# A fused mixer, PEER and transformer kernel: 768 instead of 640 gathered features, the high products of a unit ahead of its low ones, and loads and PSUM copies moved

## The chip, the cores and the metric

The kernel runs on one core of one Trainium2 chip. The metric is the device time of one execution in microseconds (us), and lower is better. Before the change, three runs took 2994.68, 3000.39 and 3007.38 us, median 3000.39. The profiled execution is a run of its own.

## The reference, cut to what matters

256 tokens of 2048 features go through two blocks, in fp32. The first block mixes the tokens (a pooling part and a recurrent part), then runs a PEER layer: each token picks 16 of 16384 experts in each of 8 heads, so 128 experts in all. The second block is attention, a convolution and a feed-forward part of 8192. The change concerns the PEER layer's second product:

```python
        gate = jax.nn.softmax(top_s, axis=-1)
        u = jnp.take(peer_u, expert, axis=0)
        act = jax.nn.gelu(jnp.einsum('chkd,cd->chk', u, zc))
        v = jnp.take(peer_v, expert, axis=0)
        w = (gate * act.astype(jnp.float32)).astype(zc.dtype)
        return jnp.einsum('chk,chkd->cd', w, v).astype(zc.dtype)
```

The result for one token is a sum of 128 rows of `peer_v`, each with its own weight. It can be computed in two ways: as a dense product of all 16384 experts with a weight matrix that is zero where an expert was not picked, or by gathering the 128 rows of each token and adding them up with their weights. The kernel does most of it densely and a part by gathering.

## The kernel before, in words

**Units and halves.** All matrix work is cut into 544 units. A unit has two halves of weights, each 128 partitions x 1024 fp32 values (512 KB). For every half, SP issues a DMA into one of 8 `raw` slots as soon as the half that used the slot 8 halves earlier has been multiplied; ACT rounds it into one of 7 `hi` slots (`prep`, L982); DVE subtracts that from the raw half and leaves the rest, `lo`, in the raw slot (L1378). PE multiplies in three products for accuracy: high by high, low by high, high by low. Each engine's program is written out in order, one unit after the other: the tables of the file (`LOAD_G_AT`, `LOAD_H_AT`, `COPY_AT`, `PHASED` and so on) say at which unit an engine issues each extra operation. Semaphores count finished steps (`s_raw`, `s_hi`, `s_lo`, `s_mm`).

**Stages.** Units 0 to 55 are the first block's projections. Units 56 to 183 are the PEER layer's first products (`u` stage, 8 chunks of 16 units), and units 184 to 311 its second products (`v` stage, again 8 chunks). Unit 312 (`F0`) starts the second block.

**The second products.** Here the output is by token: 128 tokens on the partitions, features in the columns. A unit holds four blocks of 128 experts by 512 features. Token half 0 multiplies all 512 columns. Token half 1 multiplies only the first 128 x `FROM_Q` of the 2048 features (`FROM_Q` = 11, 1408 features), and the other `WIDE` = 640 are gathered. So with q the quarter of 512 features: units of q = 0 and 1 have 512 columns for both halves, units of q = 2 have 512 and 384, units of q = 3 have 512 and nothing. Chunks 0 to 6 go through q = 0, 1, 2, 3 four times, and the last chunk has four units of q = 0, then four of q = 1, 2 and 3. A `FLIPPED` unit has its halves in `hi` slots 6 and 0, so that a piece of 384 columns can't be read in one stride: there it is cut into 256 and 128 (`pieces`). This concerns five units of q = 2.

**The gather.** `widen` (L1178, on ACT's DMA queue) copies the 640 features of all 16384 experts into a table `v_wide`, one row per expert, in 80 copies of 512 KB, at the units in `COPY_AT`. In the `v` stage, POOL issues for each of the 128 picks one indirect DMA that gathers 128 rows (L2102, into a ring of 6 blocks of two picks) and one for their activations (L2110, `asp`), 13 DMAs in 6 units. DVE adds the rows up (`picked_dot`, L1709), four units behind.

**Gates and activations.** For each chunk of the `v` stage, ACT's queue loads the gates `Gc` (L1186, four times 512 KB) and the activations (`A`, `Y` <- `h_scratch`, L1196, four times 512 KB). DVE multiplies them, ACT and DVE split them into `ZB`.

**The end of the stage.** The quarters are finished one after another in the last chunk. ACT and DVE copy them out of the PSUM (`expert_out`: ACT's copy is L1132; DVE's is L1761, and L1765 puts the gathered features in), PE transposes them (`expert_turn`, L715), DVE adds them to X (L1771), ACT squares and scales X (`expert_sum`, L1138 to L1146) and DVE makes the low part `ZA` (L1775), which unit 312 multiplies.

## Time and profile before

| | us |
|---|---|
| median of three runs | 3000.39 |
| the three runs | 2994.68, 3000.39, 3007.38 |
| profiled execution, its own time | 2997.14 |
| its span in the profile | 2995.3 |
| PE busy | 2971.8 |
| DVE busy | 2145.3 |
| ACT busy | 1565.0 |
| POOL busy | 961.1 |

The span is the time from the first to the last instruction of the profile, and the profiled execution's own time has 1.84 us around it. A busy PE is not a PE at its peak: matmuls overlap, so the pitch from one start to the next is what a matmul costs, and the duration in a row is longer. "PEclk" is the clock that TensorE was granted, as a share of its full 2.4 GHz. The "DMA share" of a stretch is the mean busy share of the core's 16 DMA engines; transfers that overlap on one engine can take it a little above 1. "q1" is the queue of SP's loads, "q10" that of ACT's, "q0" that of POOL's gathers.

### The profile page before, as it was taken

To read this page: it belongs to the slowest core of one execution; us is meant where nothing else is said; L and a number is where in the kernel's file an instruction comes from. 1 tells how busy PE (TensorE), PEld (TensorE's weight loads), DVE (VectorE), ACT (ScalarE), POOL (GpSimd) and SP (SyncE) were. 2 spreads that over 40 slices of the span, in tenths; PEclk is the share of its full clock that TensorE was granted. 3 is DMA by queue.
4 is the path that set the end of the run, shared out by engine and by line. 5 is a ranking of instruction groups with operands and counts; after the bars stand their busy time and mean duration, and the time that the engine had idled before them with its cause. 6 is when DMAs were issued, how large, how long until landed. Compare 5 with 4: busy or idle time off the path is not lost.

```text
span 2995.3 us, 42127 instructions
## 1 busy us (share of the span) xinstructions
PE 2971.8 (99%) x15968; PEld 2559.2 (85%) x15968; DVE 2145.3 (72%) x3097; ACT 1565.0 (52%) x2160; POOL 961.1 (32%) x728
## 2 busy tenths in 40 slices
PE   9999999999999999999999999999999999999999
PEld 8888888888888888888788788888888888888887
DVE  8957995555566767887778899897867855545554
ACT  7655464444444544545455656656566544434443
POOL 0022458888883055565554300000522000000000
PEclk9999999999999999999999999999999999999999
DMA  8898978999999899999997555555555565577664
GB/s 301 289 323 285 350 217 246 270 245 247 246 244 281 283 308 337 347 334 343 333 333 255 198 179 175 171 182 189 190 189 176 188 187 191 189 206 193 193 194 148
DMA packets 403194, 730.44 MB, mean 244 GB/s; under 512 B 66992, under 2 KB 226992, under 8 KB 400304
## 3 DMA queue, kind: packets, MB, share of 16 engines
q1 hardware_dynamic: 240608, 574.70, 58.8%
q10 hardware_dynamic: 111184, 110.88, 11.2%
q0 software_dynamic: 51200, 42.17, 6.5%
q8 instruction: 126, 2.06, 0.3%
q14 instruction: 76, 0.62, 0.1%
HBM read 690.80 MB, written 78.78 MB: 257 GB/s over the span
## 4 chain that ended last, share of the span: by engine, by line
PE 88%; DVE 4%; DMA 3%; issue 2%; ACT 1%; POOL 1%; SPq 0%; ACTq 0%; POOLq 0%; DVEq 0%
PE G L586 40%; PE G L590 20%; DMA raw<-in_pv 3%; PE G L656 3%; PE G L657 3%; PE G L658 3%; PE M L656 2%; PE M L658 2%; PE M L657 2%; PE G L683 2%; PE M L683 2%; PE M L684 2%; PE G L684 2%; PE M L685 2%; PE G L685 2%
## 5 line engine op out<-in xcount | busy, mean ns | idle before, releaser
L586 PE MATMUL G<-ZA,hi 128*128 128x512 f32 x5098 | 1765.7, 395 | 4.0 <-DVE lo L1378 1.5
L1378 DVE TENSOR_TENSOR lo<-raw,hi 128x1024 fp32r<-128x1024 f32 x1088 | 1338.1, 1244 | 515.7 <-ACT hi L982 485.3
L982 ACT ACTIVATE hi<-raw 128x1024 fp32r<-128x1024 f32 x1088 | 1129.9, 1055 | 615.5 <-DMA raw<-in_pv 276.6
L590 PE MATMUL G<-ZA,lo 128*128 128x256 f32 x5114 | 1389.4, 278 | 0.0
L586 PEld LDWEIGHTS G<-ZA,hi 128*128 128x128 f32 x5098 | 943.1, 188 | 211.0 <-DVE lo L1378 2.2
L590 PEld LDWEIGHTS G<-ZA,lo 128*128 128x128 f32 x5114 | 961.0, 188 | 16.7
L2086 POOL DMA_INDIRECT g_scratch<-sel,IDX x256 | 442.2, 1728 | 115.5 <-issue 82.6
L989 ACT ACTIVATE tA<-G 128x256 f32<-128x256 f32 x367 | 139.2, 380 | 508.9 <-PE G L590 488.3
L1384 DVE TENSOR_TENSOR tS<-G,tA 128x256 f32<-128x256 f32 x336 | 140.7, 419 | 262.0 <-ACT tA L989 256.7
L2102 POOL DMA_INDIRECT vrow<-v_wide,IXV x128 | 166.0, 1297 | 241.9 <-PE G L590 127.4
L656 PE MATMUL G<-hi,ZB 128*128 128x512 f32 (+3 forms) x532 | 197.9, 372 | 3.8 <-DVE lo L1378 3.8
L2110 POOL DMA_INDIRECT asp<-h_scratch,IXA x128 | 161.2, 1260 | 119.4 <-PE G L658 51.0
L657 PE MATMUL G<-lo,ZB 128*128 128x512 f32 (+3 forms) x532 | 197.8, 372 | 0.0
L658 PE MATMUL G<-hi,ZB 128*128 128x512 f32 (+3 forms) x532 | 197.6, 371 | 0.0
L586 PE MATMUL G<-ZB,hi 128*128 128x512 f32 x512 | 177.4, 394 | 1.4 <-DVE ZB L1458 1.4
L656 PE MATMUL M<-hi,ZB 128*128 128x512 f32 x384 | 151.5, 394 | 3.3 <-DVE lo L1378 3.3
L657 PE MATMUL M<-lo,ZB 128*128 128x512 f32 x384 | 150.4, 392 | 0.0
L658 PE MATMUL M<-hi,ZB 128*128 128x512 f32 x384 | 150.4, 392 | 0.0
L590 PE MATMUL G<-ZB,lo 128*128 128x256 f32 x512 | 140.9, 277 | 0.0
L1794 DVE SCALAR_TENSOR_TENSOR CV<-UC,col,CV 128x256 f32<-128x256 f32 x240 | 117.0, 488 | 6.6
L656 PEld LDWEIGHTS G<-hi,ZB 128*128 128x128 f32 x532 | 99.9, 188 | 22.1 <-DVE lo L1378 5.5
L586 PEld LDWEIGHTS G<-ZB,hi 128*128 128x128 f32 x512 | 95.6, 188 | 23.5 <-DVE ZB L1458 1.7
(368 smaller groups left out, 2779.1 us busy)
## 6 DMA issues: line engine op xcount, KB each, us to landing
raw<-in_pu SPq DMA_DIRECT2D x256, 512.0 KB
raw<-in_pv SPq DMA_DIRECT2D x256, 512.0 KB
raw<-in_w_in SPq DMA_DIRECT2D x192, 512.0 KB
raw<-in_w_up SPq DMA_DIRECT2D x128, 512.0 KB
raw<-in_w_down SPq DMA_DIRECT2D x128, 512.0 KB
v_wide<-in_pv ACTq DMA_DIRECT2D x80, 512.0 KB
raw<-in_w_out SPq DMA_DIRECT2D x32, 512.0 KB
raw<-in_wq SPq DMA_DIRECT2D x32, 512.0 KB
```

The source lines that it names most:

```text
L586: pe.matmul(G[:, 0:512], w, Z[:, k, :], start=first, stop=False, skip_group_check=True)
L590: m = pe.matmul(G[:, 0:256], lo[raw_slot(POS[u][p])][:, k % 8, :], weights(u, p)[1][:, k, 0:256], start=False, stop=last, skip_group_check ...
L656: pe.matmul(to, zhi, vhi, start=c == 0 and n == 0 and x == 0, stop=False, skip_group_check=True)
L657: pe.matmul(to, zhi, vlo, start=False, stop=False, skip_group_check=True)
L658: m = pe.matmul(to, zlo, vhi, start=False, stop=c == 7 and n == 3 and x == 3, skip_group_check=True)
L982: act.activation(hi[w][:, :, :], raw[r].rearrange("p (k n) -> p k n", k=8), ACT.Copy).then_inc(s_hi, 1)
L989: act.activation(tA[b % 3][:, :], GB[b % 4][:, 256:512], ACT.Copy).then_inc(s_low, 1)
L1378: dve.tensor_tensor(lo[r][:, :, :], raw[r].rearrange("p (k n) -> p k n", k=8), hi[w][:, :, :].bitcast(F32), ALU.subtract).then_inc(s_lo, 1)
L1384: dve.tensor_tensor(dst, GB[b % 4][:, 0:256], tA[b % 3][:, :], ALU.add).then_inc(s_join, 1)
L2086: pool.indirect_dma_start(scr, bass.IndirectOffsetOnAxis(IDX[:, t, k:k + 1], 0), sel[:, t, k:k + 1], None, compute_op=ALU.add).then_inc(s_ ...
L2102: pool.indirect_dma_start(vrow[:, slot_of(b), k, :], None, vwide, bass.IndirectOffsetOnAxis(IXV[:, at:at + 1], 0)).then_inc(s_pick[b % 2], 16)
L2110: pool.indirect_dma_start(asp[:, at:at + 1], None, hflat, bass.IndirectOffsetOnAxis(IXA[:, at:at + 1], 0)).then_inc(s_pick[b % 2], 16)
```

## The change: what it does

- `WIDE` goes from 640 to 768, so `FROM_Q` from 11 to 10. Units of q = 2 multiply 512 and 256 columns. Gathers, dots and the table become one fifth wider. `RING` goes from 6 blocks to 5. The table takes 96 copies instead of 80: 52 of them in units 4 to 39 where there were 46, and 45 in units 66 to 154 (every second unit) where there were 34 in units 66 to 165 (every third).
- `expert_unit` issues all products with high weights (zhi x vhi and zlo x vhi) of a unit first, waiting only for `s_hi`, and then all products with low weights, for which it waits for `s_lo`. `pieces` goes: 256 columns can always be read in one stride.
- Group 3 of the gates is loaded at units 178 to 181, ahead of the stage; groups 4 to 7 come at units 196, 201, 206, ... to 274, seven units behind the place that the group before had, so that no `Gc` load stands at the same unit as a load of activations.
- `PHASED` gains the second unit of each chunk of the `u` stage (8 units): its matmuls are the same, in an order that has two high products before the first low one.
- PE's third `expert_turn` comes behind unit 309 instead of 308. ACT's last `expert_out` comes at unit 310 instead of 312.

```diff
-PHASED = [19, OT + 1, MG, YO + 1, M0 + 3, M0 + 5]
+PHASED = [b + 1 for b in UB] + [19, OT + 1, MG, YO + 1, M0 + 3, M0 + 5]
...
-WIDE = 640
+WIDE = 768
...
-RING = 6
+RING = 5
...
-for _n, _u in enumerate(sorted(list(range(4, 40)) + list(range(8, 28, 2)) + list(range(66, 168, 3)))):
+for _n, _u in enumerate(sorted(list(range(4, 40)) + list(range(8, 38, 2)) + list(range(66, 156, 2)))):
...
-                               (LOAD_G_AT, 2, _m - 11), (KEPT_AT, 2, _m - 8)):
+                               (LOAD_G_AT, 2, _m - 11), (KEPT_AT, 2, _m - 8), (LOAD_G_AT, 3, _m - 6)):
...
-    for _table, _u in ((LOAD_G_AT, _u), (LOAD_H_AT, _u), (KEPT_AT, _u + 5)):
-        _table[_u] = [(3 + _j // 4, _j % 4)]
+    for _table, _group, _u in ((LOAD_H_AT, 3 + _j // 4, _u), (KEPT_AT, 3 + _j // 4, _u + 5), (LOAD_G_AT, 4 + _j // 4, _u + 7)):
+        if _group < KEPT:
+            _table[_u] = [(_group, _j % 4)]
...
+TURN_AT = (V_LAST + 4, V_LAST + 8, V_LAST + 13)
...
-                weights_ready(POS[u][1])
...
-                for x in range(4):
-                    if q == 0 and x % 2 == 0:
-                        pe.wait_ge(s_za, 8 * c + 2 * n + x // 2 + 1)
...
-                        for at, w, vhi, vlo in pieces(u, whi, wlo, x, e):
-                            to = G[:, at:at + w]
-                            pe.matmul(to, zhi, vhi, start=c == 0 and n == 0 and x == 0, stop=False, skip_group_check=True)
-                            pe.matmul(to, zhi, vlo, start=False, stop=False, skip_group_check=True)
-                            m = pe.matmul(to, zlo, vhi, start=False, stop=c == 7 and n == 3 and x == 3, skip_group_check=True)
+                pe.wait_ge(s_hi, POS[u][1] + 1)
+                for low in range(2):
+                    if low:
+                        weights_ready(POS[u][1])
+                    for x in range(4):
+                        if q == 0 and x % 2 == 0 and not low:
+                            pe.wait_ge(s_za, 8 * c + 2 * n + x // 2 + 1)
...
+                            if low:
+                                m = pe.matmul(G[:, 0:e], zhi, vlo, start=False, stop=c == 7 and n == 3 and x == 3, skip_group_check=True)
+                            else:
+                                pe.matmul(G[:, 0:e], zhi, vhi, start=c == 0 and n == 0 and x == 0, stop=False, skip_group_check=True)
+                                pe.matmul(G[:, 0:e], zlo, vhi, start=False, stop=False, skip_group_check=True)
                 m.then_inc(s_mm, 2)
...
-                if u in range(V_LAST + 4, F0, 4):
-                    expert_turn((u - V_LAST) // 4 - 1)
+                if u in TURN_AT:
+                    expert_turn(TURN_AT.index(u))
...
-                if u in range(V_LAST + 4, F0 + 1, 4):
+                if u in range(V_LAST + 4, F0, 4):
                     expert_out((u - V_LAST) // 4 - 1)
...
+                if u == V_LAST + 14:
+                    expert_out(3)
```

On PE, in unit 186 (the first of q = 2; G and M are the PSUM banks of the two token halves, `hi` and `lo` on the left of ZB the weights, and L656, L657, L658 the three products), the kernel before has for one block of experts after another, with three rows for each token half:

```order
5965 L656 MATMUL G<-hi,ZB 128x512
5966 L657 MATMUL G<-lo,ZB 128x512
5967 L658 MATMUL G<-hi,ZB 128x512
5968 L656 MATMUL G<-hi,ZB 128x384
5969 L657 MATMUL G<-lo,ZB 128x384
5970 L658 MATMUL G<-hi,ZB 128x384
```

and the changed kernel, at the unit's first matmuls and at the change from high to low:

```order
5970 L652 MATMUL G<-hi,ZB 128x512
5971 L653 MATMUL G<-hi,ZB 128x512
5972 L652 MATMUL G<-hi,ZB 128x256
5973 L653 MATMUL G<-hi,ZB 128x256
...
5982 L652 MATMUL G<-hi,ZB 128x512
5983 L653 MATMUL G<-hi,ZB 128x512
5984 L652 MATMUL G<-hi,ZB 128x256
5985 L653 MATMUL G<-hi,ZB 128x256
5986 L650 MATMUL G<-lo,ZB 128x512
5987 L650 MATMUL G<-lo,ZB 128x256
5988 L650 MATMUL G<-lo,ZB 128x512
5989 L650 MATMUL G<-lo,ZB 128x256
```

The low product (L650) of each block moved to behind all sixteen high ones (L652, L653), and the 384 columns of token half 1 became 256.

On ACT, near the start of the `v` stage, the kernel before issues a load of gates (L1186) and one of activations (L1196) at the same unit, with the splits L982 of the weights around them:

```order
937 L982 ACTIVATE hi<-raw 128x1024 x2
938 L1186 DMA Gc<-g_scratch 128x1024
939 L1196 DMA A<-h_scratch 128x1024
940 L982 ACTIVATE hi<-raw 128x1024 x6
941 L1106 ACTIVATE ZB<-A 128x2x256 x2
942 L982 ACTIVATE hi<-raw 128x1024 x4
943 L1186 DMA Gc<-g_scratch 128x1024
944 L1196 DMA A<-h_scratch 128x1024
```

and the changed kernel at the same place:

```order
952 L977 ACTIVATE hi<-raw 128x1024 x8
953 L1101 ACTIVATE ZB<-A 128x2x256 x2
954 L977 ACTIVATE hi<-raw 128x1024 x2
955 L1191 DMA A<-h_scratch 128x1024
956 L977 ACTIVATE hi<-raw 128x1024 x6
957 L1101 ACTIVATE ZB<-A 128x2x256 x2
958 L977 ACTIVATE hi<-raw 128x1024 x4
959 L1191 DMA A<-h_scratch 128x1024
960 L977 ACTIVATE hi<-raw 128x1024 x4
961 L1101 ACTIVATE ZB<-A 128x2x256 x2
962 L1181 DMA Gc<-g_scratch 128x1024
```

The two loads are now seven units apart, and the first load of gates comes two units behind the second of activations.

On ACT, at the end of the stage, `expert_sum` is the group of four rows L1138 to L1146 for one tile of 128 features, and the last copy out of the PSUM (L1132) comes in the kernel before behind the groups of tiles 10 and 11:

```order
1097 L982 ACTIVATE hi<-raw 128x1024 x2
1098 L1138 ACTIVATE tQ<-X 128x256
1099 L1139 ACTIVATE X<-X,col 128x256
1100 L1143 ACTIVATE ZA<-X,col 128x256
1101 L1146 ACTIVATE tQ<-X 128x256
1102 L982 ACTIVATE hi<-raw 128x1024 x2
1103 L1138 ACTIVATE tQ<-X 128x256
1104 L1139 ACTIVATE X<-X,col 128x256
1105 L1143 ACTIVATE ZA<-X,col 128x256
1106 L1146 ACTIVATE tQ<-X 128x256
1107 L1132 ACTIVATE A<-M 128x512
```

In the changed kernel the same stretch reads:

```order
1120 L977 ACTIVATE hi<-raw 128x1024 x2
1121 L1127 ACTIVATE A<-M 128x512
1122 L1133 ACTIVATE tQ<-X 128x256
1123 L1134 ACTIVATE X<-X,col 128x256
1124 L1138 ACTIVATE ZA<-X,col 128x256
1125 L1141 ACTIVATE tQ<-X 128x256
1126 L977 ACTIVATE hi<-raw 128x1024 x2
1127 L1133 ACTIVATE tQ<-X 128x256
1128 L1134 ACTIVATE X<-X,col 128x256
1129 L1138 ACTIVATE ZA<-X,col 128x256
1130 L1141 ACTIVATE tQ<-X 128x256
```

The copy (now L1127) stands ahead of both groups and of the two splits between them.

## Rows read from the trace of the kernel before

**Rows 1.** The page: busy us of each engine, and the chain's shares:

```profile
PE 2971.8 (99%) x15968; PEld 2559.2 (85%) x15968; DVE 2145.3 (72%) x3097; ACT 1565.0 (52%) x2160; POOL 961.1 (32%) x728
...
PE 88%; DVE 4%; DMA 3%; issue 2%; ACT 1%; POOL 1%; SPq 0%; ACTq 0%; POOLq 0%; DVEq 0%
```

**Rows 2.** Stretches: window, us, busy of PE, PEld, DVE, ACT, POOL, clock, DMA share, GB/s:

```profile
1070.00:1610.00 540.00, 532.88 (x2437) 445.80 (x2436) 428.54 (x483) 268.36 (x284) 313.80 (x246) 1.00 0.95 335
560.00:960.00 400.00, 400.00 (x2309) 349.79 (x2308) 236.18 (x290) 198.31 (x288) 308.08 (x182) 1.00 0.94 249
```

**Rows 3.** Waits between 1070 and 1610 us (us in all, times, longest):

```profile
ACT hi L982 <- DMA raw<-in_pv: 257.2, 185, 7.3
...
POOL asp L2110 <- DVE vacc L1709: 15.3, 9, 3.8
...
PE G L656 <- DVE lo L1378: 3.8, 4, 1.5
PE M L656 <- DVE lo L1378: 3.3, 5, 1.2
```

**Rows 4.** PE's timeline, a unit of q = 2 (start, us):

```profile
1141.87 0.33 PE L656 MATMUL G<-hi,ZB 128*128 128x384 f32 x1
...
1142.40 0.40 PE L656 MATMUL G<-hi,ZB 128*128 128x512 f32 x1
...
1142.86 0.39 PE L658 MATMUL G<-hi,ZB 128*128 128x512 f32 x1
```

**Rows 5.** PE's timeline, a flipped unit of q = 2:

```profile
1160.41 0.28 PE L656 MATMUL G<-hi,ZB 128*128 128x256 f32 x1
...
1160.76 0.22 PE L656 MATMUL G<-hi,ZB 128*128 128x128 f32 x1
...
1161.05 0.44 PE L656 MATMUL G<-hi,ZB 128*128 128x512 f32 x1
```

**Rows 6.** PE's group of 384 columns, 1056 to 1640 us:

```profile
L657 PE MATMUL G<-lo,ZB 128*128 128x384 f32 x98 | 33.3, 340 | 0.0
```

**Rows 7.** DMA, 1070 to 1610 us: packets, MB, share of 16 engines; issues:

```profile
q1 hardware_dynamic: 61626, 118.79, 63.9%
q0 software_dynamic: 13856, 40.71, 20.5%
q10 hardware_dynamic: 5760, 20.97, 10.0%
...
Gc<-g_scratch ACTq DMA_DIRECT2D x20, 512.0 KB
A<-h_scratch ACTq DMA_DIRECT2D x12, 512.0 KB
Y<-h_scratch ACTq DMA_DIRECT2D x8, 512.0 KB
```

**Rows 8.** View of stretches, short ones inside the second products:

```profile
1360.00:1370.00 10.00, 10.00 (x47) 8.40 (x46) 6.24 (x9) 4.11 (x5) 5.99 (x5) 1.00 1.03 393
1236.00:1266.00 30.00, 30.00 (x138) 25.34 (x137) 22.91 (x28) 13.23 (x14) 18.50 (x16) 1.00 0.99 360
```

**Rows 9.** DVE's groups between 1070 and 1610 us (busy, mean ns, idle before):

```profile
L1709 DVE SCALAR_TENSOR_TENSOR vacc<-vrow,asp,vacc 128x640 f32<-128x640 f32 x118 | 99.2, 882 | 2.1
```

**Rows 10.** DMA queues between 560 and 960 us:

```profile
q10 hardware_dynamic: 35449, 23.45, 19.6%
...
v_wide<-in_pv ACTq DMA_DIRECT2D x24, 512.0 KB
```

**Rows 11.** PE's waits at the stage's end, 1610 to 1690 us:

```profile
PE G L715 <- DVE A L1765: 3.1, 1, 3.1
PE M L715 <- ACT A L1132: 2.4, 1, 2.4
```

**Rows 12.** ACT's timeline at the stage's end:

```profile
1664.06 0.42 ACT L1138 ACTIVATE tQ<-X 128x256 f32<-128x256 f32 x1 [2.53 <-DVE X L1771]
...
1674.09 0.58 ACT L1132 ACTIVATE A<-M 128x512 f32<-128x512 f32 x1
```

More of the change, by code:

```diff
@@ L623, in half @@
                     x += step
-            def pieces(u, whi, wlo, x, e):
-                if e % 256 == 0:
-                    return [(0, e, whi[:, 0:e // 256, :, x, :], wlo[:, 0:e // 256, :, x, :])]
-                if FLIPPED[u]:
-                    return [(0, 256, whi[:, 0, :, x, :], wlo[:, 0, :, x, :]), (256, 128, whi[:, 1, 0, x, :], wlo[:, 1, 0, x, :])]
-                a, b = POS[u][0] % NW, POS[u][0] % NRAW
-                whi, wlo = (w.rearrange("p s t f -> p (s t) f").rearrange("p (q k) f -> p q k f", k=4)
-                            for w in (his[:, a:a + 2, :, :], los[:, b:b + 2, :, :]))
-                return [(0, e, whi[:, 0:e // 128, x, :], wlo[:, 0:e // 128, x, :])]
             def expert_unit(u):
@@ L645, in expert_unit @@
                 whi, wlo = (w.rearrange("p s (q k) f -> p s q k f", k=4) for w in (whi, wlo))
-                for x in range(4):
-                    if q == 0 and x % 2 == 0:
-                        pe.wait_ge(s_za, 8 * c + 2 * n + x // 2 + 1)
-                    for h, G in enumerate(VM[q]):
-                        e = min(512, max(0, 128 * (FROM_Q - 4 * q))) if h else 512
-                        if not e:
-                            continue
-                        zhi, zlo = (ZB[:, 4 * n + x, at:at + 128] for at in (128 * h, 256 + 128 * h))
-                        for at, w, vhi, vlo in pieces(u, whi, wlo, x, e):
-                            to = G[:, at:at + w]
-                            pe.matmul(to, zhi, vhi, start=c == 0 and n == 0 and x == 0, stop=False, skip_group_check=True)
-                            pe.matmul(to, zhi, vlo, start=False, stop=False, skip_group_check=True)
-                            m = pe.matmul(to, zlo, vhi, start=False, stop=c == 7 and n == 3 and x == 3, skip_group_check=True)
+                pe.wait_ge(s_hi, POS[u][1] + 1)
[5 more added lines that the diff above has]
+                            pe.wait_ge(s_za, 8 * c + 2 * n + x // 2 + 1)
+                        for h, G in enumerate(VM[q]):
+                            e = min(512, max(0, 128 * (FROM_Q - 4 * q))) if h else 512
+                            if not e:
+                                continue
+                            zhi, zlo = (ZB[:, 4 * n + x, at:at + 128] for at in (128 * h, 256 + 128 * h))
+                            vhi, vlo = whi[:, 0:e // 256, :, x, :], wlo[:, 0:e // 256, :, x, :]
+                            if low:
[3 more added lines that the diff above has]
+                                pe.matmul(G[:, 0:e], zlo, vhi, start=False, stop=False, skip_group_check=True)
                 m.then_inc(s_mm, 2)
```

## The prediction, made before the changed kernel ran

> **What bounds the kernel now.** I read the page's busy times and its chain first. PE is busy 2971.8 of 2995.3 us and makes up 88% of the chain that ended last [rows 1], so time is won only where PE has fewer columns to multiply or stops waiting, and only as long as what feeds PE keeps up. Then the view of stretches, because the average hides the stage that the change touches. In the stretch from 1070 to 1610 us (units 187 to 300, the second products) PE is busy 532.88 of 540.00 us at full clock, while the 16 DMA engines are busy to 0.95 and move 335 GB/s. From 560 to 960 us (first products) PE is busy 400.00 of 400.00 at a DMA share of 0.94 and 249 GB/s [rows 2]. The third view is the one of waits: in the second products ACT waits 257.2 us for raw weights, in 185 waits, so a half is split as soon as it has landed. What PE waits for is the low part, nine times, 3.8 and 3.3 us in all, never above 1.5 us [rows 3]. So this stage is PE-bound with the DMA close behind it. There are two questions: how many PE columns go, and whether the DMA can bring the same weights, and more gathered rows, in the shorter time.
>
> **PE's side.** Only units of q = 2 change. In an ordinary one, three matmuls of 384 columns run from 1141.87 to 1142.40, 0.177 us each [rows 4]. Three of 256 run from 1160.41 to 1160.76 in a flipped unit, 0.117 each, and its three of 128 take until 1161.05, so the six take 0.64 us [rows 5]. After, three of 256 do it. An ordinary unit has four blocks of three: 12 x (0.177 - 0.117) = 0.72 us. A flipped one gains 4 x (0.64 - 0.35) = 1.16 us. The stage has 32 units of q = 2, five of them flipped, so 27 with 384 columns: each of their three products has 98 records, where 27 x 4 = 108 were issued and a few are missing from the trace [rows 6]. Inside 1070 to 1610 stand 23 ordinary and 4 flipped units; one ordinary is unit 186, before it, and the four of the last chunk (304 to 307) come after it. So PE gains 23 x 0.72 + 4 x 1.16 = 16.6 + 4.6 = 21.2 us there. The new order of products lets a unit start with `s_hi` alone and puts the wait for the low part behind two thirds of its matmuls, 1.8 us (q = 3) to 3.6 us (q = 0 and 1) later at 0.23 us for 512 columns (1142.40 to 1142.86 for two [rows 4]). The longest of the nine waits is 1.5 us, so at an equal supply all 7.1 us go, and what is late next is the high part. The matmuls themselves are as many as before, and a changed order costs nothing by itself; I bound that at 0.1 us either way for a unit. PE alone would need 540.0 - 21.2 - 7.1 = 511.7 us.
>
> **The DMA's side.** The shares in the stretch are 63.9% for the weights, 20.5% for POOL's gathers and 10.0% for ACT's loads [rows 7], 94.4% of 540, that is 510 us of all 16 engines. The rows gathered get a fifth wider. That adds between 0 (if the cost is per row; the activations' gathers on the same queue don't grow) and 0.2 x 20.5% x 540 = 22 us (all by bytes). I take 22, since the queue's 40.71 MB are nearly all these rows. Loads of gates: 4 of the 40 loads of ACT's queue (20 of `Gc`, 12 and 8 of A and Y) move ahead of the stage, - 4/40 x 10.0% x 540 = - 5. Sum 527 us. To fit into 511.7 us the share would have to be 527 / 511.7 = 1.03, for 500 us on end. The trace has such a share for 10 us (1.03 at 393 GB/s), while the best 30 us that I found have 0.99 [rows 8], and the whole stretch has 0.95. So the price of this term lies between three points. With a share of 0.95 as before the stretch takes 527 / 0.95 = 555 us (+15). With 1.00 it takes 527 us (-13). With 1.03 PE decides and it takes 511.7 (-28). I take 1.00: PE set the pace before, so the 0.95 was demand and no ceiling; the later wait for the low parts and the loads that no longer coincide allow a longer queue; and 1.00 is nearest to the 30 us row. The stretch gives **-13**.
>
> By the Trainium skill, DMA: Bandwidth & Descriptors, section Where 436 GB/s comes from, HBM gives a core some 358 GB/s. The bytes of the stretch are 118.79 + 40.71 + 20.97 = 180.5 MB, and with a fifth more gathered rows and four loads fewer 186.5 MB, an estimate by that page of 521 us, so -19 instead of -13. The trace agrees as far as a mean of 335 goes, and has 393 for 10 us, so as a ceiling for short stretches the figure doesn't hold here.
>
> **Wider rows elsewhere.** DVE has 118 dots of 882 ns there [rows 9]; at a fifth wider, 0.18 us more at most (all of it by columns), 128 x 0.18 = 23 us over the stage. DVE is busy 428.54 of 540 [rows 2]: 428.5 + 21 = 450 of 527, hidden behind its idle time, and delays of the low parts lie inside the 1.8 to 3.6 us that the new order gives. With the old order they would have gone to PE. At the end of the stage a pair of dots and the wider add stand on DVE's path: +0.4. Unit 186 gives -0.7, a flipped 304 -1.2.
>
> **Copies of the table.** 11 more fall into the first products, every second unit in place of every third. All of ACT's queue has 19.6% of 400 us there = 78 us, with 24 copies in it besides other traffic [rows 10], so a copy costs at most 3.3 us and the 11 at most 36 us; they are issued over 88 units, some 490 us (2309 matmuls in 400 us at 32 for a unit make 5.5 us a unit [rows 2]), and would lift the share from 0.94 to at most 1.01. I take half. PE doesn't wait there in 400 us [rows 2], so 0; if the cover is gone, up to +10. The five more copies in the first block: 0 to +3, taken 0.
>
> **The ring of 5, the loads of gates, PHASED.** A pick waits for the dots of the block five before in place of six. Blocks come every 1.85 units (13 DMAs in 6 units, 4 for a block) and dots four units behind, so the slot is free 5 x 1.85 - 4 = 5.2 units (some 25 us) ahead; POOL waited for dots 15.3 us in 9 waits, 3.8 at most [rows 3]. 0, bounds 0 and +2. The gates' load sits on ACT ahead of splits; at its new unit its slot is longer free than before: 0, bounds -2 and +1 (the first of them beyond what the DMA term has). The 8 new PHASED units have the same matmuls: 0, bounds -1 and +1.
>
> **End of the stage.** PE waited 3.1 us for DVE's copy ahead of the third transposes and 2.4 us for ACT's last copy [rows 11]. With the transposes a unit of q = 3 later (2.7 us) the first wait nearly goes, and PE has unit 309 done sooner. But the end of this stage is the chain of copies, adds and `expert_sum`, which feeds unit 312: ACT stood idle until DVE's add at 1664.06 and copied the last bank at 1674.09 [rows 12]. PE's time saved in 305 to 311 is given back there, so those three q = 2 units count 0. The last copy moves ahead of two groups of four instructions of about 0.4 us each and of splits; DVE's add of that bank stands where it stood. I take 0, bounds -4 (the last bank is ready so much sooner) and +3 (ACT stands at the copy until unit 311 is done and its groups are late).
>
> **Sum.** -13 - 0.7 - 1.2 + 0.4 = -14.5. From the profiled execution's 2997.14 us (span 2995.3 and 1.8 around it) this is 2982.6. The profiled run lies 3.25 us below the median of 3000.39, so against that median 2985.9. I predict **2985 us**, between the two.
>
> **Rivals.** (1) *The DMA keeps up and PE decides.* For it: the 10 us rows at 1.03, and that shares above 1 only mean overlapping transfers. Against it: nothing in the trace holds it for 30 us. Time: -28 in place of -13, 2968 to 2971 us. (2) *The DMA has no more than its mean, slower.* The place is the same stretch: the weights' queue shares engines with a fifth more gathered bytes; from a share below 527 / 540 = 0.976 the stage is longer than before, and at 0.95 it is +15 - 1.5: 3011 to 3014 us. For it: the share is 0.95 and ACT already waits for weights half the stretch. Against it: 0.99 for 30 us with PE never waiting in them. (3) *The cover in the first products or at the stage's end is gone:* copies at +10 or ACT's copy at +3 beside the -14.5: some 2991 to 2998 us. (4) *The change doesn't do what it says:* the low waits turn into waits for the high parts one for one, so the 7.1 us stay and the share stays near 0.97: 2998 us, no change.
>
> **Chances.** Forecast (share 0.98 to 1.02): 0.45. Rival 1: 0.24. Rival 2: 0.12. Rivals 3 and 4 together: 0.19. A measurement of this kernel can tell 0.5%, 15 us, from no change, so faster means below some 2985. The forecast sits on that bound and gives 0.22 to each side, rival 1 is all faster, rival 2 mostly slower: faster 0.46, same 0.43, slower 0.11. The range leaves out the outer half of rival 1 and of rival 2: 2964 to 3007 us. The forecast's own range (share 0.98 to 1.02) is 2975 to 2996.
>
> **What would show it.** Right: PE has no 384-column group; the units of q = 2 are 0.7 us shorter; the stretch of units 187 to 300 lasts some 527 us with a DMA share near 1.00; PE's waits are for ACT's `hi` or few for `lo`; the first products keep 400.00 of 400.00. Rival 1 shows as a stretch of 512 us without waits, rival 2 as PE waits of over 30 us in it with a share still at 0.95. Wrong altogether would be waits in the first products, or a stage's end that is longer by more than 3 us.

## The result: 2969.5 us, one per cent faster, twice the gain forecast

Four runs of the changed kernel took 2967.06 to 2971.44 us, median 2969.48, against a median of 2999.88 us before (four runs). The ratio is 0.9895 with a 95% interval of 0.9875 to 0.9914. The forecast was 2985, so its sign was right, the size half of what came, and the numbers are those of rival 1. The profiled execution took 2971.44 us, 25.7 us less than the one before (2997.14).

The page of the profile after, for [rows 1] (busy us of each engine, and the chain's shares):

```profile
PE 2946.2 (99%) x15908; PEld 2535.8 (85%) x15908; DVE 2160.1 (73%) x3097; ACT 1567.5 (53%) x2160; POOL 984.2 (33%) x728
...
PE 89%; DVE 4%; DMA 2%; issue 2%; ACT 1%; POOL 1%; SPq 0%; ACTq 0%; POOLq 0%; DVEq 0%
```

PE is still the bound, with 25.6 us less of it. Where they went shows in ACT's timeline: the first split of unit 188 and that of unit 300, first in the kernel before, then after.

```profile
1065.27 1.06 ACT L982 ACTIVATE hi<-raw 128x1024 fp32r<-128x1024 f32 x1 [3.37 <-DMA raw<-in_pv]
...
1596.84 1.06 ACT L982 ACTIVATE hi<-raw 128x1024 fp32r<-128x1024 f32 x1 [0.24 <-DMA raw<-in_pv]
```

```profile
1065.71 1.06 ACT L977 ACTIVATE hi<-raw 128x1024 fp32r<-128x1024 f32 x1 [3.20 <-DMA raw<-in_pv]
...
1570.85 1.06 ACT L977 ACTIVATE hi<-raw 128x1024 fp32r<-128x1024 f32 x1 [0.43 <-DMA raw<-in_pv]
```

From 531.6 us the distance fell to 505.1: 26.4 us, the whole difference and 0.7 more. So the stretch that was 1070 to 1610 us is 1070 to 1584 us now. The view of stretches after, for [rows 2], with one piece of 85 us:

```profile
1070.00:1584.00 514.00, 509.13 (x2389) 424.44 (x2389) 442.63 (x483) 268.04 (x284) 340.99 (x247) 1.00 1.01 364
...
1245.00:1330.00 85.00, 85.00 (x404) 71.14 (x403) 76.65 (x84) 46.51 (x50) 53.87 (x42) 1.00 1.03 377
```

```profile
560.00:960.00 400.00, 400.00 (x2308) 349.70 (x2308) 239.51 (x292) 200.41 (x290) 305.29 (x183) 1.00 0.95 259
```

The first products are as they were: 400.00 us of 400.00, with the denser copies at a DMA share of 0.95 after 0.94. In the second products the DMA engines held 1.01 and 364 GB/s for 514 us, and for 85 us 1.03 and 377 GB/s with no wait of PE. The waits in that stretch, for [rows 3] (us in all, times, longest):

```profile
ACT hi L977 <- DMA raw<-in_pv: 245.4, 196, 4.7
...
PE M L652 <- ACT hi L977: 2.5, 4, 1.0
PE M L650 <- DVE lo L1375: 2.4, 2, 1.5
POOL asp L2107 <- DVE vacc L1706: 2.1, 3, 1.5
```

PE waits 4.9 us where it waited 7.1, now half for the high part. POOL waits less for dots with the smaller ring, not more. The DMA queues there, for [rows 7], and DVE's dots, for [rows 9]:

```profile
q1 hardware_dynamic: 61729, 119.00, 65.7%
q0 software_dynamic: 13856, 48.84, 24.9%
q10 hardware_dynamic: 5184, 18.88, 9.6%
```

```profile
L1706 DVE SCALAR_TENSOR_TENSOR vacc<-vrow,asp,vacc 128x768 f32<-128x768 f32 x118 | 115.0, 1016 | 2.1
```

A dot takes 0.134 us more (0.18 was the bound). POOL's queue moves the fifth more. At the stage's end PE's waits are, for [rows 11]:

```profile
PE G L588 <- DVE lo L1375: 4.7, 1, 4.7
PE G L710 <- DVE A L1758: 2.9, 1, 2.9
PE G L588 <- DVE ZA L1772: 1.3, 2, 0.7
```

The wait for ACT's last copy (2.4 us) is gone, and a wait of 4.7 us for the low part of unit 312 has come. PE's clock fell at this end as well. The view of stretches has these two after, and under them the only one of its kind there before:

```profile
1611.00:1616.00 5.00, 4.59 (x20) 4.15 (x21) 4.96 (x7) 2.12 (x2) 0.00 (x0) 0.66 0.41 156
1642.00:1650.00 8.00, 5.68 (x23) 5.01 (x24) 6.23 (x7) 7.94 (x15) 4.45 (x5) 0.57 0.18 72
```

```profile
1659.00:1663.00 4.00, 4.00 (x15) 3.23 (x14) 4.00 (x5) 1.76 (x2) 0.00 (x0) 0.57 0.38 153
```

The granted clock is the mean of a stretch in which it stood partly at 2.4 and partly at 1.2 GHz. Each of the three lies at a long wait of PE: 2.9 us until 1611.41 and 4.7 us until 1644.32 after, 3.15 us until 1658.43 before. From unit 299 to the program's end the profiled execution takes 1.4 us more than before, though four units of q = 2 with fewer columns lie in it.

### The profile page after: what moved, and what is told of

It reads as the page before. It is cut to its first block, busy times and chain, and to the rows that moved or that the text cites. A ratio compares the mean times of both kernels' runs of the same rounds, so it can differ in the third digit from the quotient of the medians.

```text
span 2969.6 us, 42024 instructions
## 1 busy us (share of the span) xinstructions
PE 2946.2 (99%) x15908; PEld 2535.8 (85%) x15908; DVE 2160.1 (73%) x3097; ACT 1567.5 (53%) x2160; POOL 984.2 (33%) x728
## 4 chain that ended last, share of the span: by engine, by line
PE 89%; DVE 4%; DMA 2%; issue 2%; ACT 1%; POOL 1%; SPq 0%; ACTq 0%; POOLq 0%; DVEq 0%
PE G L588 40%; PE G L592 20%; PE M L650 3%; PE G L652 3%; PE G L653 3%; PE G L650 3%; PE M L652 3%; PE M L653 3%; DMA raw<-in_pv 2%; PE G L679 2%; PE M L679 2%; PE M L680 2%; PE G L680 2%; PE M L678 2%; PE G L678 2%
## 5 line engine op out<-in xcount | busy, mean ns | idle before, releaser
L2099 POOL DMA_INDIRECT vrow<-v_wide,IXV x128 | 179.6, 1403 | 218.1 <-PE G L592 129.2
L2107 POOL DMA_INDIRECT asp<-h_scratch,IXA x128 | 173.8, 1358 | 91.6 <-PE G L650 33.4
L652 PE MATMUL G<-hi,ZB 128*128 128x512 f32 (+1 forms) x512 | 182.1, 364 | 0.0
L653 PE MATMUL G<-hi,ZB 128*128 128x512 f32 (+1 forms) x512 | 180.3, 364 | 0.0
L652 PE MATMUL M<-hi,ZB 128*128 128x512 f32 x384 | 150.2, 391 | 2.5 <-ACT hi L977 2.5
L653 PE MATMUL M<-hi,ZB 128*128 128x512 f32 x384 | 149.6, 390 | 0.0
L1706 DVE SCALAR_TENSOR_TENSOR vacc<-vrow,asp,vacc 128x768 f32<-128x768 f32 x126 | 123.5, 1021 | 2.2
L650 PE MATMUL G<-lo,ZB 128*128 128x512 f32 (+1 forms) x512 | 112.8, 362 | 0.0
L653 PEld LDWEIGHTS G<-hi,ZB 128*128 128x128 f32 x512 | 96.8, 189 | 16.9
```

Of the source, the lines that this page charges most:

```text
L650: m = pe.matmul(G[:, 0:e], zhi, vlo, start=False, stop=c == 7 and n == 3 and x == 3, skip_group_check=True)
L652: pe.matmul(G[:, 0:e], zhi, vhi, start=c == 0 and n == 0 and x == 0, stop=False, skip_group_check=True)
L653: pe.matmul(G[:, 0:e], zlo, vhi, start=False, stop=False, skip_group_check=True)
L2099: pool.indirect_dma_start(vrow[:, slot_of(b), k, :], None, vwide, bass.IndirectOffsetOnAxis(IXV[:, at:at + 1], 0)).then_inc(s_pick[b % 2], 16)
L2107: pool.indirect_dma_start(asp[:, at:at + 1], None, hflat, bass.IndirectOffsetOnAxis(IXA[:, at:at + 1], 0)).then_inc(s_pick[b % 2], 16)
```

## Experiments

They were measured in three groups of four, in the order in which they stand here, each group on one chip and together with runs of the kernel before (the first and the third group on the same chip). Within a group the times can be set against each other to some 2 us; the kernel before had a median of 2998.84, 2997.46 and 2998.72 us in them. The changed kernel itself ran ahead of them, in none of the groups.

**1. The order of products alone, on the kernel before.**

```diff
-                weights_ready(POS[u][1])
+                pe.wait_ge(s_hi, POS[u][1] + 1)
+                for low in range(2):
+                    if low:
+                        weights_ready(POS[u][1])
...
```

> The kernel before with one part of the change: the products with high weights of a unit first, then those with low weights, behind their own wait. Columns, gather, loads and the stage's end as before. Theory A (the order takes the nine low waits and nothing else): the 7.1 us of waits in the second products go, 2993 us, 0.2% faster, PE waits for low parts gone there. Rival (the high part is as late as the low one was): the waits only change their name, 3000 us.

Median 2990.65 us (12 runs), before 2998.84 in this group: ratio 0.9981 (0.9968 to 0.9993, which is 2 to 10 us). The profile has no wait of PE in the second products at all. Theory A holds, 7 us forecast and 8 measured. Four of the twelve runs took 3000.6 to 3002.5, the other eight 2988.7 to 2992.7, and the profiled one is among the four; more on that in the last section.

**2. The old order on the changed kernel.**

```diff
-                pe.wait_ge(s_hi, POS[u][1] + 1)
-                for low in range(2):
-                    if low:
-                        weights_ready(POS[u][1])
...
+                weights_ready(POS[u][1])
+                for x in range(4):
...
+                        pe.matmul(to, zhi, vhi, start=c == 0 and n == 0 and x == 0, stop=False, skip_group_check=True)
+                        pe.matmul(to, zhi, vlo, start=False, stop=False, skip_group_check=True)
+                        m = pe.matmul(to, zlo, vhi, start=False, stop=c == 7 and n == 3 and x == 3, skip_group_check=True)
```

> The changed kernel with the order of products of before (high-high, high-low, low-high for each block, one wait for the low part at the unit's start); everything else as changed. Theory A (PE's columns decide, the DMA engines have room, and the order is worth about the waits that were there): 5 to 8 us longer than the changed kernel, some 2976 us. Theory B (at a DMA share above 1.00 landings come so late that the low parts are late in far more units, and the later wait is what hides it): 15 us or more longer, 2985 us or above, with more than 20 us of PE waits for low parts in the second products.

2987.78 us (6 runs), ratio 0.996 (0.9945 to 0.9975), 18 us above the changed kernel and 17 above the fourth kernel of the same group. PE's waits in this execution, and the stretch:

```profile
PE M L647 <- DVE lo L1371: 16.2, 19, 2.5
```

```profile
1070.00:1584.00 514.00, 500.21 (x2324) 413.59 (x2323) 430.92 (x469) 260.55 (x275) 324.73 (x240) 1.00 0.99 355
```

Theory B has the time, though its row of waits is below 20 us: 19 waits, 16.2 us, none longer than 2.5. The changed kernel has 4.9 us. The rest of the 15 us by which the two profiled executions differ is not seen in the rows of waits, but it hangs on them: a wait costs more than its row shows (see the table behind experiment 12), and one of 2.33 us is followed by matmuls at half the clock:

```profile
1370.10 0.63 PE L647 MATMUL M<-hi,ZB 128*128 128x512 f32 x1 [2.33 <-DVE lo L1371]
```

```profile
1370.00:1375.00 5.00, 4.90 (x14) 3.87 (x15) 3.39 (x4) 2.11 (x2) 1.98 (x2) 0.66 0.97 366
```

The order, which I had priced at 7.1 us, is worth 17 or 18 at the new pace. Waits of 2.5 us at most lie mostly within the 1.8 to 3.6 us that the later wait gives.

**3. The gates' loads where they were.**

```diff
-                               (LOAD_G_AT, 2, _m - 11), (KEPT_AT, 2, _m - 8), (LOAD_G_AT, 3, _m - 6)):
+                               (LOAD_G_AT, 2, _m - 11), (KEPT_AT, 2, _m - 8)):
...
+    for _table, _u in ((LOAD_G_AT, _u), (LOAD_H_AT, _u), (KEPT_AT, _u + 5)):
+        _table[_u] = [(3 + _j // 4, _j % 4)]
```

> The changed kernel with the loads of gates where they were before: groups 3 to 7 inside the stage, at the same units as the loads of activations. Theory A (the engines have room): 0 to 2 us longer than the changed kernel. Rival (two loads of 512 KB at once are what makes the weights late): 5 us or more longer, with PE waits in units 189 to 288 near the loads.

2973.98 us (5 runs), ratio 0.9913 (0.9898 to 0.9929). That is 2.9 us above the fourth kernel and 4.5 above the changed one, between theory A and its rival, and the intervals of the three overlap. Its profile shows 1.7 us of waits for the high part and 1.8 us for the low in the second products, fewer than the 4.9 of the changed kernel, and units 185 to 299 take 520.4 us where the changed kernel takes 520.9. The 1.9 us by which this execution is the longer one lie ahead of that: by the end of unit 184 it is 2.5 us late, 1.5 us of it by unit 56, and in that first block the view of stretches has the clock at 0.66 from 166 to 171 us (1.00 in the changed kernel), behind a wait of 1.99 us for ZB. So no cost of the loads' place is shown; the medians bound it at some 3 to 4 us.

**4. The stage's end as before.**

```diff
-TURN_AT = (V_LAST + 4, V_LAST + 8, V_LAST + 13)
+TURN_AT = (V_LAST + 4, V_LAST + 8, V_LAST + 12)
...
-                if u in range(V_LAST + 4, F0, 4):
+                if u in range(V_LAST + 4, F0 + 1, 4):
...
-                if u == V_LAST + 14:
-                    expert_out(3)
```

> The changed kernel with the third transposes behind unit 308 and ACT's last PSUM copy at unit 312, as before. My step (the chain of copies, adds and sums sets the end of the stage, PE's order doesn't): within 1 us of the changed kernel. Rival (the earlier copy is what won): 2 to 4 us longer. In the profile: the wait at the third transposes is 3 us or more again, and ACT's last copy comes some 3 us later.

2971.13 us (5 runs), ratio 0.99 (0.9884 to 0.9915), 1.6 us above the changed kernel, which is between the step and its rival and within what runs of different groups differ. The waits are those of before and longer, and still cost nothing that can be measured (from unit 299 to the end 1389.2 us against 1388.3):

```profile
PE G L710 <- DVE A L1760: 5.3, 1, 5.3
PE G L710 <- DVE A L1756: 3.3, 1, 3.3
PE M L710 <- ACT A L1127: 2.4, 1, 2.4
```

**5. 640 gathered, everything else as changed.**

```diff
-WIDE = 768
+WIDE = 640
...
-RING = 5
+RING = 6
...
+                            for at, w, vhi, vlo in pieces(u, whi, wlo, x, e):
```

> The changed kernel with 640 gathered features, a ring of 6 and the 80 copies of before; 384 columns in units of q = 2, pieces again, everything else as changed (order of products, gates' loads, PHASED, end). Both theories: PE's columns are back, 23 x 0.72 + 4 x 1.16 + 2 = 23 us longer than the changed kernel, some 2991 us, and like the order alone on the kernel before.

2988.93 us (11 runs), ratio 0.9969 (0.996 to 0.9978). It is 21 us above the eighth kernel, of the same group, where 23 were forecast.

**6. The bytes without the columns.**

```diff
-                                e = min(512, max(0, 128 * (FROM_Q - 4 * q))) if h else 512
+                                e = (512, 512, 384, 0)[q] if h else 512
```

> The changed kernel, 768 features gathered, but units of q = 2 still multiply 384 columns of the second token half (the 128 columns too many are computed and not used). Against the kernel with 640 and 384 this adds the bytes and nothing for PE. Theory A (the DMA engines have room at this pace): the same within 1.5 us, some 2991 us, DMA share near 0.99. Theory B (more gathered bytes make weights late in themselves): 4 us or more longer than it.

2990.45 us (12 runs), ratio 0.9977 (0.9967 to 0.9986): 1.5 us more than with 640. At this pace a fifth more gathered bytes cost next to nothing, at a share of 0.99 after 0.97. In the profiled executions units 185 to 299 take 538.5 us with either; what the wider rows cost (3.2 us there) lies behind unit 299. Theory A.

**7. The columns without the bytes.**

```diff
-WIDE = 768
+WIDE = 640
...
+                                e = (512, 512, 256 if c else 384, 0)[q] if h else 512
```

> The changed kernel with 640 gathered features, a ring of 6 and 80 copies, but units of q = 2 multiply only 256 columns of the second token half from chunk 1 on; features 1280 to 1407 of that half get the products of chunk 0 alone, the rest of them is left out. This takes PE's columns without the bytes. Theory A (PE decides, the bytes cost nothing): 20 x 0.72 + 4 x 1.16 = 19 us shorter than the kernel with 640 and 384, so some 2972 us, and the changed kernel itself (four more units cut) lies 2 to 3 us below it. Theory B (the bytes took a part of the gain): this one is 2 us or more below the changed kernel, 2967 us or less.

2966.41 us (5 runs), ratio 0.9896 (0.9879 to 0.9914). This kernel leaves out a part of the products, so it is a measure and no rival. The columns took 22.5 us (forecast 19), and PE has no wait in units 185 to 299. In theory A the kernel with 768 would be 2.9 us below this one (four more units cut, 0.72 each); it is 1.4 us above (experiment 8, same group) and 3.1 above (the changed kernel). So the bytes take back 4 to 6 us of some 25. Both theories have a share: A in the main, B for the rest.

**8. Without the new PHASED units.**

```diff
-PHASED = [b + 1 for b in UB] + [19, OT + 1, MG, YO + 1, M0 + 3, M0 + 5]
+PHASED = [19, OT + 1, MG, YO + 1, M0 + 3, M0 + 5]
```

> The changed kernel without the 8 new PHASED units. From the look at the order alone on the kernel before: PE's matmuls in the first products stood 176.7 ns apart on average in that execution, 173.3 in the others, without a wait, from about unit 88 to 184. Theory P (the two high products at the start of every chunk end such a state): without them some executions have it, 5 to 13 us longer, so the runs spread over more than 6 us, and the median is 0 to 3 us above the changed kernel. Rival (the state comes from something else, or the units do nothing): runs within 5 us of each other, median within 1 us of the changed kernel.

2967.79 us (2967.0 to 2969.4, 5 runs), ratio 0.9898 (0.9881 to 0.9915). Nothing of theory P shows: the rival.

**9. 896 gathered.**

```diff
-WIDE = 768
+WIDE = 896
...
-RING = 5
+RING = 4
...
+                            vhi, vlo = (w[:, 0:e // 256, :, x, :] if e > 128 else w[:, 0, 0, x, :] for w in (whi, wlo))
```

> One step further than the change: 896 features gathered, units of q = 2 multiply 512 and 128 columns, a ring of 4, 112 copies of the table (58 of them in units 66 to 180). By the pitches (0.117 us for 256 columns, 0.097 for 128) PE saves 12 x 0.02 = 0.24 us a unit, 6.5 us in 27. The DMA engines get another 17 us of transfers in the stretch of units 187 to 300, 517 + 17 = 534 us against a stretch of 507. Theory A (no ceiling met yet): 3 to 6 us shorter than the changed kernel, share 1.05. Theory C (a ceiling of about 1.03): the stretch takes 519 us, the kernel 5 us or more longer than the changed one, with PE waits of more than 15 us for weights.

2977.91 us (5 runs), ratio 0.9937 (0.9923 to 0.995), 9.4 us above the kernel of experiment 11. The stretch, a piece of 85 us, PE's waits, and the matmuls of a unit of q = 2:

```profile
1070.00:1584.00 514.00, 505.86 (x2370) 418.37 (x2369) 453.07 (x479) 265.39 (x281) 310.64 (x244) 1.00 1.02 376
...
1330.00:1415.00 85.00, 84.10 (x394) 69.06 (x393) 76.82 (x81) 43.78 (x47) 51.22 (x41) 1.00 1.04 386
```

```profile
PE M L650 <- DVE lo L1375: 5.7, 4, 1.9
...
PE M L652 <- ACT hi L977: 3.7, 5, 1.8
```

```profile
1084.74 0.22 PE L652 MATMUL G<-hi,ZB 128*128 128x128 f32 x1
1084.80 0.28 PE L653 MATMUL G<-hi,ZB 128*128 128x128 f32 x1
1084.91 0.45 PE L652 MATMUL G<-hi,ZB 128*128 128x512 f32 x1
...
1085.42 0.22 PE L652 MATMUL G<-hi,ZB 128*128 128x128 f32 x1
```

The time is theory C's (5 us or more longer), the reason only in part. Two of 512 and two of 128 columns take 0.68 us (1084.74 to 1085.42); with 256 in the changed kernel they take 0.70 (below). My 0.02 us a matmul was not there, since the 512 columns behind two of 128 start 0.28 us apart instead of 0.23: one step more of columns saves PE almost nothing. Over a whole unit of q = 2 it is 0.10 us, and the unit of q = 3 behind it is 0.07 us longer. PE's waits in the second products are 9.8 us in all by their rows (9.4 in the two shown), not over 15; units 185 to 299 take 9.7 us more than with the same ring and 768 (experiment 11), which is nearly the whole loss. The DMA moved 376 GB/s in the stretch, more than in the changed kernel. So 896 loses because more weights land late and almost no columns pay for it; that 1.03 or 1.04 is a ceiling is not shown.

```profile
1138.08 0.28 PE L652 MATMUL G<-hi,ZB 128*128 128x256 f32 x1
1138.19 0.28 PE L653 MATMUL G<-hi,ZB 128*128 128x256 f32 x1
...
1138.78 0.28 PE L652 MATMUL G<-hi,ZB 128*128 128x256 f32 x1
```

**10. The PHASED units on the kernel before.**

```diff
-PHASED = [19, OT + 1, MG, YO + 1, M0 + 3, M0 + 5]
+PHASED = [b + 1 for b in UB] + [19, OT + 1, MG, YO + 1, M0 + 3, M0 + 5]
```

> The kernel before with the 8 PHASED units alone. Of 39 runs of the kernel before six took more than 3001 us, of 12 with the new order alone four took 10 us more than the others, and of 48 runs of kernels with the 8 units none did. Theory P: no run over 3001 us, median 2997 us. Rival (chance, or another part of the change): one run in six or more is some 5 to 12 us above the rest.

2997.94 us (2993.19 to 3004.60, 11 runs), ratio 1.0001 (0.9992 to 1.001). One run is over 3001, so theory P's forecast failed as it was put. The median doesn't move. In the same group the kernel before had two runs over 3010 and this one none, which is too few to tell.

**11. A ring of 4.**

```diff
-RING = 5
+RING = 4
```

> The changed kernel with a ring of 4 blocks instead of 5, the control for the kernel with 896 gathered features, which has 4 too. Slots come free 4 x 1.85 - 4 = 3.4 units ahead of their use: within 1 us of the changed kernel. Rival (gathers held up by dots bunch up and push the weights): 3 us or more longer, with POOL waiting for DVE's dots much more than 2 us in all.

2968.47 us (4 runs), ratio 0.9906 (0.9891 to 0.9921). The time didn't move, though POOL waits for dots far more often:

```profile
POOL vrow L2099 <- DVE vacc L1706: 85.5, 32, 4.5
```

A wait of POOL is no wait of PE here: the gathers come 4.5 us later at most, and are still in time.

**12. The old order at 768 and 384.**

```diff
-                                e = min(512, max(0, 128 * (FROM_Q - 4 * q))) if h else 512
+                        e = (512, 512, 384, 0)[q] if h else 512
...
+                weights_ready(POS[u][1])
```

> The changed kernel with 768 gathered and 384 multiplied columns (as run above, 2990 us) and the old order of products. It tells why the order is worth 18 us at 768 and 256 and 8 us on the kernel before. Theory B1 (it is the bytes): waits for low parts of 12 us or more, some 3002 to 3008 us. Theory B2 (it is PE's faster pace, which asks for weights sooner than they land): 7 to 10 us of waits, some 2998 us.

3001.23 us (11 runs), ratio 1.0001 (0.9987 to 1.0014), 10.8 us above the same kernel with the new order (another group), with 8 waits of PE for low parts in the second products, 7.6 us in all. The ratios 1.0001 and 0.9977 give 7 us. The time lies between the two theories (2998 and 3002); the waits are those of B2, and so is the stretch: units 185 to 299 take 9.4 us more than with the new order (547.9 and 538.5; the clock stood at 0.72 from 1342 to 1348 us, around a wait of 2.6) where with 640 gathered features they take 9.5 more (548.0 and 538.5). So the bytes alone don't raise what the order is worth. It is 7 to 11 us at 384 columns, and 17 to 18 where PE's pace is faster as well. Whether the faster pace alone does it, without the bytes, no run shows: the old order with 640 gathered and 256 multiplied features wasn't run.

**Where the time lies in each profiled execution.** The last matmul of unit 184 and that of unit 299 can be found in every trace. In the kernel before they are these:

```profile
1060.36 0.39 PE L658 MATMUL M<-hi,ZB 128*128 128x512 f32 x1
...
1608.38 0.39 PE L658 MATMUL M<-hi,ZB 128*128 128x512 f32 x1
```

The table has, in us, what lies ahead of the first, between the two (units 185 to 299) and behind the second, and PE's waits between the two as rows show them.

| kernel | ahead | units 185 to 299 | behind | waits in rows |
|---|---|---|---|---|
| before | 1060.4 | 548.0 | 1386.9 | 7.1 |
| changed | 1060.3 | 520.9 | 1388.3 | 4.9 |
| 1, order alone | 1072.4 | 538.5 | 1388.9 | 0 |
| 2, old order | 1061.2 | 536.3 | 1387.5 | 13.8 |
| 5, 640 | 1060.4 | 538.5 | 1386.6 | 0 |
| 6, 768 and 384 | 1061.5 | 538.5 | 1389.8 | 0 |
| 7, 640 and 256 | 1061.4 | 517.2 | 1385.8 | 0 |
| 8, no new PHASED | 1060.6 | 518.2 | 1388.8 | 2.4 |
| 9, 896 | 1060.9 | 525.8 | 1388.7 | 8.1 |
| 11, ring of 4 | 1060.4 | 516.1 | 1388.1 | 0.8 |
| 12, old order at 384 | 1063.1 | 547.9 | 1388.6 | 5.3 |

If each unit takes the shortest time that it took in any execution with the same matmuls in the same order, the middle part is 538.2 us for the kernel before and 513.9 for the changed one. So late weights cost the kernel before 9.8 us, where nine rows of waits add up to 7.1, and the changed one 7.0 us in this execution, where six rows add up to 4.9. That makes some 0.3 us for each wait that its row doesn't show. A part of it is how rows count: a wait begins at the end of a matmul's row, 0.39 us behind its start, but the next matmul could have started 0.23 us behind it. The changed kernel and its four variants with the same matmuls in this stretch (experiments 3, 4, 8 and 11) spread from 516.1 to 520.9, so late weights cost them 2 to 7 us from one execution to the next.

## Why the prediction was off by a factor of two

**PE's side: right, a little small.** The columns gave 22.5 us in 28 units (experiment 7) where 19 were worked out, and the waits went as said. The profile has the pitches as forecast: two of 512 and two of 256 columns in 0.70 us (experiment 9). What was missed is small for each unit: an ordinary unit of q = 2 together with the unit of q = 3 behind it went from 7.68 to 6.90 us (experiment 5 and the changed kernel, from last matmul to last matmul, without waits), 0.78 us where 0.72 was worked out, and a flipped one gained 1.41 us in place of 1.16. For experiment 7 this makes 20 x 0.78 + 4 x 1.41 = 21.2 us, and the table shows 21.3 in units 185 to 299.

**The step that failed is the DMA term, "I take 1.00":** the stretch was said to last as long as its 527 us of transfers, at a share of 1.00. It turned 28 us of gain into 13. The share did come out at 1.00 to 1.01, but the stretch lasted 514 us. What the runs show instead is that PE set the pace, and that the bytes cost PE 1.5 us at the old pace (experiment 6) and 4 to 6 at the new one (experiment 7), where the step charged 15. In units 185 to 299 that is 2 to 7 us of late weights (the table above); the rest of it lies behind unit 299. Two things were wrong in the step. First, the sum of 527 us took the engines' busy time per byte as fixed. It isn't. The weights' queue took 63.9% of 540 us for 118.79 MB before, 2.90 us a MB [rows 7], and after 65.7% of 514 us for 119.00 MB, 2.84; the gathers went from 2.72 us a MB (20.5% of 540 us for 40.71 MB) to 2.62 (24.9% of 514 us for 48.84 MB). So a MB took 2 to 4% less busy time, and the demand came out at 515 us by the three queues (100.2% of 514) and 519 by the view of stretches (1.01). For the weights the packets are the same; the gathers moved their 48.84 MB in as many packets as the 40.71 before (13856), so with them a cost that goes by row is a second cause: at PE's old pace they took 2.73 us a MB with 640 features and 2.63 with 768 (experiments 5 and 6). With 640 features at the fast pace (experiment 7), the weights' queue had this:

```profile
q1 hardware_dynamic: 62328, 120.14, 67.6%
```

This is 2.89 us a MB, and with 896 (experiment 9) it was 2.80:

```profile
q1 hardware_dynamic: 61289, 118.15, 64.3%
```

So the weights' cost a MB fell as the core's traffic rose, 2.89 at 351 GB/s, 2.84 at 364 and 2.80 at 376, and a share of 0.95 was no measure of what was left. Why it falls, the traces don't tell; that a transfer is open for longer than it needs is one reading. Second, the best 30 us of the trace were read as what can be held. They showed what PE had asked for, since PE didn't wait in them (busy 30.00 of 30.00 us [rows 8]).

**The figure of 358 GB/s** (the Trainium skill, DMA: Bandwidth & Descriptors, Where 436 GB/s comes from), weighed beside the sum, doesn't hold as a ceiling here, with one core running: 364 GB/s for 514 us after, 376 with 896 features.

**The order was priced by the waits it removed, 7.1 us.** At the old pace that was nearly right (8 us, experiment 1; 9.5 in units 185 to 299). At the new one it is worth 17 to 18 (experiment 2): 19 low parts would be late, nearly all of them by less than the later wait forgives. With the old order the same columns and bytes take 2988 us, close to my forecast of 2985. So the forecast, by luck, was close to a kernel that lacked this part. The two parts are worth more together: 8 us for the order alone, 11 for the columns, bytes and the rest alone (2999 to 2988), 29 to 30 for both. The text named this cover ("with the old order they would have gone to PE") and gave it no number.

**The sum of the misses.** The profiled executions differ by 25.7 us where 14.5 were forecast. In units 185 to 299 the gain is 27.1 us where the terms make 13.7 (-13 and unit 186's -0.7): 8 us of the difference is the DMA term (15 charged, 7.0 lost to late weights in this execution), 5 us is that columns and vanished waits were worth 34 and not 29. Behind unit 299 the sum had -0.8 (-1.2 for unit 304, +0.4 for the wider rows) and 1.4 us were lost. With the changed kernel's end, the kernels with 768 gathered features take 1387.5 to 1389.8 us there, and those with 640 take 1386.6 and 1385.8 (experiments 5 and 7): the wider rows cost some 2 to 3 us at the stage's end, not 0.4. What remains between 25.7 and the 30 us of the medians is which executions were profiled.

**Elsewhere:** wider dots hidden in the stretch (0.134 us each), the copies at 0 with the first products untouched, the ring at 0 (experiment 11 even with 4), the new places of the third transposes and the last copy at 0 (experiment 4), PHASED at 0 (experiment 8), the gates' loads at 3 to 4 us at most with nothing shown in the profile (experiment 3, bound -2). Rival 1 had the size: it expected the DMA to keep up, and it did but for the 4 to 6 us. That its 2968 to 2971 us were met to the microsecond is partly luck: a PE side that was 5 us too small made up for late weights that it put at nothing. Rivals 2 to 4 are out: PE waits 4.9 us, nothing was lost in the first products, and 1.4 us at the stage's end.

None of the kernels that do all the work beats the changed one by more than runs differ (2967.8 and 2968.5 in experiments 8 and 11 against 2969.5).

## What to carry to other kernels

A DMA share near 1 in a stretch where the engines that it feeds hardly wait says what was asked for and not what can be had; ask instead how many us a MB takes, and test it with a kernel that moves the bytes without speeding up the rest, and one that speeds up the rest without the bytes. An order that lets a unit start on what is there first should be priced at the pace after the change, by how many landings would then be late by less than it forgives, and not by the waits of the trace before. Rows of waits count too little: a wait costs PE some 0.3 us more than its row here, and several of the long ones here (2.0 to 4.7 us) had a stretch at half the clock beside or behind them. The distance between two matmuls that every kernel has shows the whole. Before shrinking a matmul by another step, look at the pitch of the whole pattern: behind 128 columns next to nothing was saved here.

## What was unexpected

In the profiled execution of experiment 1, PE ran 2% slower in most of the first products, at full clock and without a wait. Its timeline there, and under it that of the kernel before:

```profile
700.72 0.40 PE L586 MATMUL G<-ZA,hi 128*128 128x512 f32 x1
...
702.49 0.40 PE L586 MATMUL G<-ZA,hi 128*128 128x512 f32 x1
```

```profile
700.83 0.39 PE L586 MATMUL G<-ZA,hi 128*128 128x512 f32 x1
...
702.56 0.40 PE L586 MATMUL G<-ZA,hi 128*128 128x512 f32 x1
```

Five pairs of 512 and 256 columns take 1.77 us there and 1.73 here. From 575 to 800 us the view of stretches has 1275 matmuls in that execution, at a granted clock of 1.00, where the kernel before has 1301:

```profile
575.00:800.00 225.00, 225.00 (x1275) 195.15 (x1275) 130.51 (x159) 110.57 (x160) 186.38 (x114) 1.00 0.96 242
```

```profile
575.00:800.00 225.00, 225.00 (x1301) 196.75 (x1300) 132.59 (x162) 111.82 (x161) 188.44 (x112) 1.00 0.94 245
```

It cost some 12 us by unit 184 (1072.4 us against 1060.4 in the table), and four of the twelve runs of that kernel are longer by this much. Neither the order of products nor the loads differ in those units, and nothing waits. Whether the PHASED units keep PE out of this slower pace stays open, and so does its cause: none of the kernels with them showed it as clearly, the changed kernel without them didn't in five runs, and with them the kernel before still had a run of 3004.6 us. It matters for reading times: the kernel before spreads over 18 us and the changed one over 4 to 5.
